# Six pairs of projection tiles in a hybrid decoder kernel: half-width block products in place of full tile products

## The chip, the cores and the metric

The kernel runs on one core of one Trainium2 chip. A core has TensorE (PE in the profile: matrix products from SBUF into the 8 banks of PSUM), VectorE (DVE), ScalarE (ACT), GpSimd (POOL) and SyncE (SP, which issues the weight transfers). Each engine works through its own instructions in order, and they meet through semaphores. The metric is the device time of one execution in microseconds (us), the median of several. Everything is float32.

## The reference, cut to what matters

Two decoder layers run over 256 prompt tokens and 32 sample tokens together, T = 288 columns. Each layer begins with one projection of the normalised input, `proj = h @ w_in`, with `h` of 288 x 1024 and `w_in` of 1024 columns in and some 9,000 out. Its columns are cut into the inputs of three token mixers:

```
hq, hf, hi, hg = jnp.split(proj[..., OFF_HG:OFF_SSM], 4, axis=-1)
fgate = lb + (1.0 - lb) * jax.nn.sigmoid(hf.astype(jnp.float32))
o_hg, s_hg = hgrn2_recurrence(heads(jax.nn.silu(hq)), heads(1.0 - fgate),
                              heads(jnp.log(fgate)), heads(hi), hg_s0)
y_hg = (rms_norm(o_hg, hg_norm) * jax.nn.silu(heads(hg).astype(jnp.float32)))
ssm = proj[..., OFF_SSM:OFF_ATT]
z = ssm[..., :SSM_WIDTH]
```

After the mixers come an output projection and a channel mixer: a dense one after layer 0, one of 8 experts after layer 1.

## The kernel before, in words

Features lie on the 128 partitions, tokens along the free axis. The input `hT` is 8 blocks of 128 features x 288 tokens. A projection tile `t` is 128 output features: 8 matmuls of 128x128 weights against 128x288 tokens, summed in one PSUM bank (`proj_tile`, L1078). Tiles 0 to 3 are hq, 4 to 7 hf, 8 to 11 hi, 12 to 15 hg, 16 to 19 z, 20 to 27 the convolved inputs, and so on up to tile 69. One weight slab of 1 MB holds two tiles; a ring of four slabs is refilled by SyncE when the second tile of a slab is done.

TensorE's order is written out: after the tile `t`, `small_products(L, t)` runs what belongs there. After tile 14 it turns hi into token rows (`value_rows`), after tile 15 it turns the convolution's state rows; after tiles 19, 21, 23, ... 33 come the products of the eight levels of the recurrence (`level`), and after tile 20 those of the level called "same".

ScalarE empties each bank in the order of the tiles (its `mixer`), and does the exponentials, logarithms and tanh in between. VectorE's order in this stretch is `hgrn_inputs` and then `hgrn_levels`. `hgrn_inputs` gates hq, adds 1 to exp(-hf) (`plus`, signal hg_plus), scales to the forget gate (four instructions), clamps it, waits for its logarithm, runs four cumulative sums, forms the first level's distances (`level_dist`), and gates hg. `hgrn_levels` is for each level `i`: two multiplications (signals lvl_q and lvl_k, for which TensorE's level `i` waits), the distances for level `i + 1`, from level 2 on a quarter of the convolution for one tile, and the masks that take the level's products out of PSUM. Level `i` begins when TensorE has done level `i - 1`. In layer 0, VectorE first builds masks and constants, before `hgrn_inputs`.

GpSimd does nothing between its setup and the end of the levels; then it forms the decayed keys (L943, L944), scales states (L951, L975) and weighs decays (L968).

The dense channel mixer of layer 0 already works in the way that the change brings to the projection: `fast_pair` (L1710) computes two tiles by seven products of half width, `put` being one matmul. There VectorE forms the sums of weight blocks.

Of the kernel before, what the change touches and what calls it, by code (L numbers as in the profile page):

```python
# [8 lines left out]
ALU = mybir.AluOpType  # L9
# [3 lines left out]
P = 128  # L13
# [54 lines left out]
GATE0 = 46  # L68
NKEY = 128 + 4 * 128 + 4 * 64 + AG * TS
# [24 lines left out]
def hybrid_decoder(nc, x_prompt, x_sample, state_hgrn, state_ssm, state_conv, cache_kv_w128, cache_kv_w512,  # L94
# [6 lines left out]
    with ctx:  # L101
# [35 lines left out]
        spread = view(over, 34 * T, 6, P)  # L137
# [191 lines left out]
        sums_done, tokens_ready, part_summed, part_kept = map(sem, ("sums_done", "tokens_ready", "part_summed", "part_kept"))  # L329
# [35 lines left out]
        def plan_mixer(L):  # L365
            job(("norm", L, 0), 0)
            for t in range(N_PROJ):
                acc_job(("proj", L, t))
# [160 lines left out]
        def sums_ready(i, k):  # L529
            return sums_done, 4 * min(i, N_PAIR) + 5 * max(i - N_PAIR, 0) + k  # L530
# [51 lines left out]
        def plan_slabs(L):  # L582
            for s in range(NS_HG + NS_SSM):
                add_slab(("proj", L, 2 * s + 1), (0, rows_of(w_in[L], 0, KT, 256 * s, 256)))
# [279 lines left out]
        def _(pool):  # L864
# [66 lines left out]
            for L in range(DEPTH):  # L931
# [8 lines left out]

                pool.wait_ge(*at("kd_decay", L))
                pool.wait_ge(*filled(("lvl", L, 7, 0)))
                step(gp.tensor_tensor(kt[:, :, 0:TP], hgp[:, 4:8, 0:TP], dist[:, :, 0:TP], ALU.mult))  # L943
                say(gp.tensor_tensor(fourfold(spread[:, 0:4, :]), tail_of(hgp[:, 4:8, :]), tail_of(dist), ALU.mult),  # L944
# [79 lines left out]
        def _(pe):  # L1024
# [61 lines left out]

            def proj_slab(L, keys, nk, src):
# [37 lines left out]
            def level(L, i):  # L1125
                if i == "same":
                    kk, qq = hgp[:, 4:8], hgp[:, 0:4]
                    pe.wait_ge(*at("hg_gated", L))
# [34 lines left out]
            def decayed_keys(L):  # L1163
                pe.wait_ge(*at("kd_ready", L))
                for b in range(3):
                    yield from token_rows(("kdtok", L, b), kt, b, range(HH), 0)
# [87 lines left out]
            def ssd_x_rows(L):  # L1254
                pe.wait_ge(*at("xs_ready", L))
                pe.wait_ge(*at("vexp_ready", L, 2))
                for b in range(3):
                    yield from token_rows(("xtok", L, b), xs, b, range(4), 0)

            def ssd_b_rows(L):  # L1260
# [11 lines left out]
                yield from token_rows(("btok", L, 2), xs, 2, (4, 5), 4)  # L1272
# [326 lines left out]
            def mixer(L):  # L1599
                for t in range(N_PROJ):  # L1600
                    run(proj_tile(L, t))
# [108 lines left out]
            def fast_pair(i, sums_of, b11, b21, b22):  # L1710
# [4 lines left out]
                h = KT // 2  # L1715

                def product(out, w, x, fresh):
                    for k in range(h):
                        ins = put(out, w[:, k, :], x[:, k, :], fresh and k == 0, k == h - 1)
                    return ins  # L1720
# [62 lines left out]
            def dense(L):  # L1783
# [16 lines left out]
                pe.wait_ge(tokens_ready, 1)  # L1800
# [4 lines left out]
                for q in range(KT // 2):  # L1805
                    for c, (k0, n) in enumerate(CHUNKS):
                        take_slab(4 * n, P)
                        if q == 0:
                            pe.wait_ge(tokens_ready, 2 + c)
# [161 lines left out]
        def _(act):  # L1971
# [218 lines left out]

            def mixer(L):
# [5 lines left out]
                for t in range(N_PROJ):  # L2197
# [13 lines left out]
                    elif t < 16:  # L2211
                        out = halve_out if t < 4 or t >= 12 else copy_out
                        if t == 11:
                            act.wait_ge(*filled(key))
                            step(fn(hgp[:, t, :], psum(key)[:, 0:T], ACT.Copy))
                            empty(fn(fourfold(spread[:, 0:4, :]), tail_of(hgp[:, 8:12, :]), ACT.Copy), key)
                        else:
                            out(hgp[:, t, :], key, psum(key)[:, 0:T])
                    elif t < 20:
                        halve_out(zT[:, t - 16, :], key, psum(key)[:, 0:T])  # L2220
# [20 lines left out]
                    if t == 15:  # L2241
                        say(fn(kt, hgp[:, 12:16, :], ACT.Tanh), "hg_exp", L, 3)
# [4 lines left out]
                    if t == 19:  # L2247
                        say(fn(zexp, zT, ACT.Tanh), "z_exp", L)
# [1121 lines left out]
```

## Time and profile before

| | |
|---|---|
| median of three runs | 2108.63 us (2107.93 to 2115.63) |
| the profiled execution | 2107.59 us, of which the span of the core is 2105.8 us |
| TensorE busy | 2071.3 us, 98% of the span |
| VectorE / ScalarE / GpSimd busy | 734.9 / 400.1 / 103.8 us |
| mixer of layer 0, tiles 2 to 35 | 29.7 to 178.9 us |
| the same of layer 1 | 734.0 to 881.3 us |
| dense channel mixer | about 500 to 729 us |
| experts | from about 1224 us |

The profile is one execution. Its parts are read like this: a row of the order of time has start, duration, engine, line and operation, what is written and what is read, the shapes, the count where equal instructions were merged, and in brackets the idle time in front and what ended it. PE MATMUL records come two to a matmul, since a float32 matmul is two instructions in the trace. Several instructions go through one line of a helper (L1042 for all matmuls, L2468 for all of VectorE's tensor_tensor, L1992 for ScalarE), so shapes tell them apart.

### The profile page before, as it was taken

The page shows a single profiled execution, that of the slowest core. Times are in us where ns is not written, and L with a number is a line of the kernel's source. Part 1 is how long each engine was busy: PE and PEld are TensorE (multiplying, and loading weights), DVE is VectorE, ACT ScalarE, POOL GpSimd, SP SyncE. Part 2 cuts the span into 40 slices and gives each one's busy share as a digit, 9 for nine tenths or more (in the row PEclk, how much of TensorE's full clock was granted, in tenths as well). Part 3 has the DMA queues.
Part 4 walks back from the last instruction along what each step waited for, and adds up shares of the span by engine and source line. Part 5 has one row for each costly group of instructions (what it writes and reads, how often), then busy time and mean ns, then how long its engine had stood idle before and what let it go on. Part 6 is the DMA issues. An engine that isn't in the chain of part 4 may idle for free.

```text
span 2105.8 us, 45046 instructions
## 1 busy us (share of the span) xinstructions
PE 2071.3 (98%) x19989; PEld 1326.1 (63%) x19989; DVE 734.9 (35%) x1437; ACT 400.1 (19%) x762; POOL 103.8 (5%) x160
## 2 busy tenths in 40 slices
PE   7999999999999999999999999999999999999998
PEld 5777777778999977777777734344443434343435
DVE  5386333545677627743254311010101010101013
ACT  3423424311220123334342120000000000000000
POOL 3001020000000000011200010000000000000001
PEclk9999999999999999999999999999999999999999
DMA  5434544785554443454466699999999999999996
GB/s 167 133 108 127 181 126 133 203 258 163 161 152 147 154 131 121 122 166 125 150 190 201 233 363 412 409 411 409 412 411 410 413 405 415 402 416 394 410 415 264
DMA packets 287990, 548.77 MB, mean 261 GB/s; under 512 B 12883, under 2 KB 218501, under 8 KB 271348
## 3 DMA queue, kind: packets, MB, share of 16 engines
q1 hardware_dynamic: 279808, 535.85, 70.5%
q10 hardware_dynamic: 6644, 5.58, 0.9%
q0 software_dynamic: 1344, 4.45, 0.5%
q8 instruction: 158, 2.59, 0.5%
q14 instruction: 36, 0.29, 0.0%
HBM read 527.15 MB, written 22.50 MB: 261 GB/s over the span
## 4 chain that ended last, share of the span: by engine, by line
PE 94%; DVE 2%; DMA 1%; issue 1%; POOL 1%; ACT 1%; POOLq 0%; DVEq 0%; ACTq 0%
PE bank L1042 91%; PE bank L1048 3%; DMA mem<-in_w_moe_down_dram 1%; ACT mem L1992 1%; DVE mem L2468 0%; DVE mem L2791 0%; DVE mem L2472 0%; DVE hflat L2501 0%; POOL quarterm L915 0%; DVE mem L2817 0%; POOL lmask L891 0%; POOL lmask L893 0%; DVE col L2824 0%; DVE hflat L2468 0%; DVE mem L2828 0%
## 5 line engine op out<-in xcount | busy, mean ns | idle before, releaser
L1042 PE MATMUL bank<-mem 128*32 128x256 f32 (+10 forms) x12904 | 1047.3, 390 | 13.0 <-issue 4.2
L1042 PEld LDWEIGHTS bank<-mem 128*32 128x32 f32 (+2 forms) x12904 | 636.1, 126 | 407.8 <-issue 234.5
L1042 PE MATMUL bank<-hflat,mem 128*128 128x288 f32 (+4 forms) x2784 | 629.0, 385 | 0.9 <-ACT hflat L1992 0.7
L1042 PEld LDWEIGHTS bank<-hflat,mem 128*128 128x128 f32 (+2 forms) x2784 | 479.4, 188 | 122.5 <-issue 12.2
L1992 ACT ACTIVATE mem<-bank 128x288 f32<-128x288 f32 (+5 forms) x411 | 174.0, 428 | 834.6 <-PE bank L1042 770.2
L1042 PE MATMUL bank<-mem,steps 128*32 128x384 f32 (+1 forms) x3072 | 289.8, 539 | 0.0
L1042 PEld LDWEIGHTS bank<-mem,steps 128*32 128x32 f32 x3072 | 94.8, 110 | 191.7 <-issue 190.9
L2468 DVE TENSOR_TENSOR mem<-mem 128x512 f32<-128x512 f32 (+10 forms) x280 | 191.8, 711 | 28.6 <-PE bank L1042 18.5
L2472 DVE SCALAR_TENSOR_TENSOR hflat<-hflat,bank 128x512 f32<-128x512 f32 x24 | 15.1, 683 | 410.5 <-ACT hflat L1992 410.5
L1992 ACT ACTIVATE hflat<-bank 128x512 f32<-128x512 f32 (+1 forms) x40 | 19.6, 553 | 562.9 <-PE bank L1042 562.9
L1992 ACT ACTIVATE mem<-mem 128x1152 f32<-128x1152 f32 (+7 forms) x127 | 93.4, 737 | 107.2 <-DVE mem L2546 71.6
L1048 PE MATMUL bank<-ident,mem 128*128 128x128 f32 (+3 forms) x503 | 70.9, 280 | 12.6 <-DMA mem<-in_x_sample_dram 7.4
L2472 DVE SCALAR_TENSOR_TENSOR mem<-mem,bank 128x288 f32<-128x288 f32 (+1 forms) x73 | 34.1, 486 | 138.1 <-ACT mem L1992 100.1
L1048 PEld LDWEIGHTS bank<-ident,mem 128*128 128x128 f32 (+3 forms) x503 | 58.1, 145 | 27.8 <-issue 11.9
L2475 DVE SCALAR_TENSOR_TENSOR mem<-mem,bank 128x384 f32<-128x384 f32 (+2 forms) x45 | 18.4, 438 | 107.6 <-PE bank L1042 106.9
L1992 ACT ACT_TABLE_LOAD x41 | 52.6, 1283 | 17.4 <-issue 11.1
L2468 DVE TENSOR_TENSOR mem<-mem,bank 128x256 f32<-128x256 f32 (+2 forms) x92 | 37.5, 407 | 34.7 <-PE bank L1042 32.3
L998 POOL DMA_INDIRECT mem<-yslots,mem x6 | 5.9, 978 | 836.7 <-PE bank L1042 835.2
L2475 DVE SCALAR_TENSOR_TENSOR hflat<-hflat,bank 128x512 f32<-128x512 f32 x24 | 15.1, 683 | 83.8 <-PE bank L1042 83.8
L2472 DVE SCALAR_TENSOR_TENSOR mem<-mem 128x288 f32<-128x288 f32 (+3 forms) x45 | 25.4, 565 | 27.7 <-ACT mem L1992 26.3
L2625 DVE SCALAR_TENSOR_TENSOR mem<-mem,vecs 128x312 f32<-128x312 f32 x48 | 26.1, 545 | 1.7
L2563 DVE COPY_PREDICATED mem<-lmask,bank 128x512 f32<-128x512 uint32 (+1 forms) x32 | 21.6, 675 | 11.7 <-PE bank L1042 10.7
(244 smaller groups left out, 676.7 us busy)
## 6 DMA issues: line engine op xcount, KB each, us to landing
mem<-in_w_moe_up_dram SPq DMA_DIRECT2D x64, 2048.0 KB, 20.9
mem<-in_w_moe_down_dram SPq DMA_DIRECT2D x56, 2048.0 KB, 21.9
mem<-in_w_moe_up_dram SPq DMA_DIRECT2D x32, 2304.0 KB, 22.8
mem<-in_w_in_dram SPq DMA_DIRECT2D x70, 1024.0 KB, 5.3
mem<-in_w_moe_up_dram SPq DMA_DIRECT2D x16, 1536.0 KB, 21.9
mem<-in_w_ffn_up_dram SPq DMA_DIRECT2D x44, 512.0 KB, 5.1
mem<-in_cache_kv_w_dram SPq DMA_DIRECT2D x26, 512.0 KB, 4.9
mem<-in_cache_kv_w_dram SPq DMA_DIRECT2D x74, 128.0 KB, 4.7
```

What stands on the lines that cost most here:

```text
L998: return gp.indirect_dma_start(dst, None, src, bass.IndirectOffsetOnAxis(ap=slots, axis=0), bounds_check=last_row, oob_is_err=False)
L1042: return mm(out, lhsT, rhs, start=start, stop=stop, skip_group_check=True)
L1048: return nc.tensor.transpose(out, in_, ident[0:k, 0:k])
L1992: return nc.scalar.activation(out, in_, f, **kw)
L2468: return ve.tensor_tensor(out, a, b, op)
L2472: return ve.scalar_tensor_tensor(out, tanh, 1.0, b, ALU.add, ALU.mult)
L2475: return ve.scalar_tensor_tensor(out, a, 0.5, b, ALU.mult, op)
L2563: empty(ve.copy_predicated(a[0:n], mk, src), key)
L2625: ins = ve.scalar_tensor_tensor(cv[:, m, 0:CW], xpad[:, m, j:j + CW], w[j], cv[:, m, 0:CW], ALU.mult, ALU.add)
```

## The change

For pairs 4 to 9 (tiles 8 to 19) the input features are cut into two halves of four blocks and the tokens into two halves of 144 (TH). A pair's weights are then a 2x2 array of blocks, w11, w12 (first feature half; first and second tile) and w21, w22, the inputs a 2x2 array too, and the 8 products of the plain way become 7:

```diff
+            def proj_pair(L, t):
+                p, h = t // 2, KT // 2
...
+                (a11, a12), (_, a22) = quarters(slab(n_slab[0], KT, 2 * P))
+                t1, t2, t3, t4 = (tok_m[:, j] for j in range(4))
+                s1, s2, s3, s4 = (msum[SEVEN.index(p) % 2][:, j] for j in range(4))
...
+                if t % 2 == 0:
+                    a = open_bank(("piece", L, p, 0))
+                    product(third(a, 0), a11, hT[:, 0:h, 0:TH], True)
+                    product(third(a, 1), a12, hT[:, h:KT, 0:TH], False)
+                    pe.wait_ge(*at("hg_plus", L, 1))
+                    close_bank(product(third(a, 2), a22, t4, False), ("piece", L, p, 0))
+                    pe.wait_ge(*mixer_sums(L, p, 1))
+                    product(third(open_bank(("piece", L, p, 1)), 0), s1, t1, True)
+                    return
+                b = psum(("piece", L, p, 1))
+                pe.wait_ge(*mixer_sums(L, p, 2))
+                product(third(b, 1), s2, t2, False)
+                pe.wait_ge(*mixer_sums(L, p, 3))
+                close_bank(product(third(b, 2), s3, t3, False), ("piece", L, p, 1))
+                c = open_bank(("piece", L, p, 2))
+                pe.wait_ge(*mixer_sums(L, p, 4))
+                close_bank(product(third(c, 0), s4, hT[:, h:KT, TH:T], True), ("piece", L, p, 2))
```

A `product` is four matmuls of 128x128 against 128x144. GpSimd forms the four sums of weight blocks of a pair, each 128x512, into one of two buffers. It starts on pair 4 when ScalarE has done the first tanh (hg_exp 1), and on pair p + 2 when TensorE has finished pair p:

```diff
+                for i, p in enumerate(SEVEN):
+                    n = first_slab[L] + p
+                    pool.wait_ge(slab_in[n % RING], 16 * slab_dmas[n])
+                    if i >= 2:
+                        pool.wait_ge(*filled(("piece", L, SEVEN[i - 2], 2)))
...
+                    if i == 0:
+                        pool.wait_ge(*at("hg_exp", L, 1))
+                    gp.tensor_tensor(s[0], w21, w22, ALU.add).then_inc(sums_done, 1)
+                    pool.wait_ge(*mixer_sums(L, p, 1))
+                    gp.tensor_tensor(s[1], s[0], w11, ALU.subtract).then_inc(sums_done, 1)
+                    gp.tensor_tensor(s[2], w11, w21, ALU.subtract).then_inc(sums_done, 1)
+                    pool.wait_ge(*mixer_sums(L, p, 2))
+                    gp.tensor_tensor(s[3], w12, s[1], ALU.subtract).then_inc(sums_done, 1)
+                    pool.wait_ge(*mixer_sums(L, p, 4))
```

ScalarE copies the seven pieces of a pair to SBUF, in three instructions (432, 432 and 144 columns) in place of two of 288. It may only write pair p + 2 when VectorE has joined pair p:

```diff
+            def keep_pieces(L, t):
...
+                if t % 2 == 0 and i >= 2:
+                    act.wait_ge(*pair_joined(L, SEVEN[i - 2]))
+                for piece in ((0,), (1, 2))[t % 2]:
+                    key, n = ("piece", L, p, piece), 1 if piece == 2 else 3
+                    out(parts[i % 2][:, 3 * piece:3 * piece + n, :].rearrange("p j t -> p (j t)"), key,
+                        psum(key)[:, 0:n * TH])
```

VectorE forms the four sums of input blocks (`pair_sums`, 128x576 each) after the first gating, and joins the pieces of each pair by five additions. Where the joins stand, and what else moves on VectorE:

```diff
+            def join_pair(L, p):
...
+                dve.wait_ge(*drained(("piece", L, p, 2)))
+                step(tt(s[:, 4], s[:, 4], s[:, 0], ALU.add))
+                step(tt(s[:, 5], s[:, 5], s[:, 4], ALU.add))
+                step(tt(dst[:, 1], s[:, 5:6].to_broadcast([P, 2, TH]), s[:, 2:4], ALU.add))
+                step(tt(s[:, 3], s[:, 3], s[:, 4], ALU.add))
+                ins = tt(dst[:, 0], s[:, 0:4:3], s[:, 1:7:5], ALU.add)
+                if p == 5:
+                    step(ins)
+                    ins = ve.tensor_copy(fourfold(spread_v), tail_of(hgp[:, 8:12, :]))
...
             def hgrn_inputs(L):
...
                 step(sigmoid_times(hgp[:, 0:4, :], qt, hgp[:, 0:4, :]))
+                h = KT // 2
+                pair_sums(tok_m, hT[:, 0:h, 0:TH], hT[:, 0:h, TH:T], hT[:, h:KT, 0:TH], hT[:, h:KT, TH:T])
...
+                join_pair(L, 4)
                 dve.wait_ge(*at("hg_log", L))
...
                 level_dist(L, 0)
-                dve.wait_ge(*at("hg_exp", L, 3))
-                say(sigmoid_times(hgp[:, 12:16, :], kt, hgp[:, 12:16, :]), "hg_gated", L)
-
+                join_pair(L, 5)
+                join_pair(L, 6)
...
+                join_pair(L, 7)
+                join_pair(L, 8)
...
                     if i == 0:
                         level_mask(L, "same")
-                    if i == 1:
+                        join_pair(L, 9)
+                        dve.wait_ge(*at("hg_exp", L, 3))
+                        say(sigmoid_times(hgp[:, 12:16, :], gate_temp, hgp[:, 12:16, :]), "hg_gated", L)
+                    if i == 3:
                         dve.wait_ge(*at("z_exp", L))
                         say(sigmoid_times(zT, zexp, zT), "z_gated", L)
```

TensorE's `value_rows` (after tile 14) waits for the join of pair 5 instead of ScalarE's copies; its level "same" waits for lvl_k 1 instead of the gating of hg; ScalarE's tanh of hg moves from tile 15 to tile 17, that of z from 19 to 22. Buffers are moved to make room, and in the dense part one semaphore is replaced by others that say the same.

On GpSimd, between the setting to zero of three arrays and the decayed keys of layer 0, before:

```order
L937 MEMSET mem 128x512
L938 MEMSET mem 128x512
L939 MEMSET mem 32x128
L943 TENSOR_TENSOR mem<-mem 128x4x256
L944 TENSOR_TENSOR mem<-mem 128x512
```

and after the change:

```order
L959 MEMSET mem 128x512
L960 MEMSET mem 128x512
L961 MEMSET mem 32x128
L972 TENSOR_TENSOR mem<-mem 128x512
L974 TENSOR_TENSOR mem<-mem 128x512
L975 TENSOR_TENSOR mem<-mem 128x512
L977 TENSOR_TENSOR mem<-mem 128x512
L972 TENSOR_TENSOR mem<-mem 128x512
```

Twenty-four sums (the last four lines stand six times) now lie in a stretch in which GpSimd had none.

On VectorE, from the gating of hq in layer 0 (the first row) to the first level's distances, before:

```order
L2472 SCALAR_TENSOR_TENSOR mem<-mem 128x1152
L2479 TENSOR_SCALAR mem<-mem 128x1152
L2513 TENSOR_SCALAR mem<-mem,lb 128x288 x4
L2515 TENSOR_SCALAR mem<-mem 128x1152
L2516 TENSOR_SCALAR mem<-mem 128x1152
L2519 SCALAR_TENSOR_TENSOR mem<-reset,mem 128x288 x4
L2468 TENSOR_TENSOR mem<-mem 128x1152
L2546 SCALAR_TENSOR_TENSOR mem<-mem 128x1152
```

and after the change:

```order
L2549 SCALAR_TENSOR_TENSOR mem<-mem 128x1152
L2545 TENSOR_TENSOR mem<-hflat 128x576 x2
L2545 TENSOR_TENSOR mem<-hflat,mem 128x576 x2
L2556 TENSOR_SCALAR mem<-mem 128x1152
L2609 TENSOR_SCALAR mem<-mem,lb 128x288 x4
L2611 TENSOR_SCALAR mem<-mem 128x1152
L2612 TENSOR_SCALAR mem<-mem 128x1152
L2545 TENSOR_TENSOR mem<-mem 128x144 x2
L2545 TENSOR_TENSOR mem<-mem 128x288
L2545 TENSOR_TENSOR mem<-mem 128x144
L2545 TENSOR_TENSOR mem<-mem 128x288
L2616 SCALAR_TENSOR_TENSOR mem<-reset,mem 128x288 x4
```

The four sums of inputs come in front of hg_plus (now L2556), and a join in front of the cumulative sums (now L2616); the join of pair 5 follows the first level's distances.

On VectorE, from the masks of "same" to the multiplications of level 1, before:

```order
L2563 COPY_PREDICATED mem<-ident,bank 128x512 x2
L2563 COPY_PREDICATED mem<-ident,bank 32x128
L2468 TENSOR_TENSOR mem<-mem 128x1152 x3
L2546 SCALAR_TENSOR_TENSOR mem<-mem 128x1152
```

and after the change:

```order
L2661 COPY_PREDICATED mem<-ident,bank 128x512 x2
L2661 COPY_PREDICATED mem<-ident,bank 32x128
L2545 TENSOR_TENSOR mem<-mem 128x144 x2
L2545 TENSOR_TENSOR mem<-mem 128x288
L2545 TENSOR_TENSOR mem<-mem 128x144
L2545 TENSOR_TENSOR mem<-mem 128x288
L2549 SCALAR_TENSOR_TENSOR mem<-mem 128x1152
L2545 TENSOR_TENSOR mem<-mem 128x1152 x3
```

The join of pair 9 and the gating of hg now stand between the masks and the two multiplications for which TensorE's level 1 waits.

## Rows read from the trace of the kernel before

**Rows 1.** The page: busy digits of 40 slices, TensorE and VectorE.
```profile
PE   7999999999999999999999999999999999999998
DVE  5386333545677627743254311010101010101013
```
**Rows 2.** Order of time, layer 0: copies of tiles 12 and 13; dense mixer: one product.
```profile
72.75 0.41 ACT L1992 ACTIVATE mem<-bank 128x288 f32<-128x288 f32 x1 [0.33 <-PE bank L1042]
76.63 0.41 ACT L1992 ACTIVATE mem<-bank 128x288 f32<-128x288 f32 x1 [3.47 <-PE bank L1042]
...
518.67 1.14 PE L1042 MATMUL bank<-hflat,mem 128*128 128x144 f32 x8
...
525.53 1.14 PE L1042 MATMUL bank<-hflat,mem 128*128 128x144 f32 x8
```
**Rows 3.** Order of time, layer 1, from tile 7's copy to the cumulative sums.
```profile
757.58 0.41 ACT L1992 ACTIVATE mem<-bank 128x288 f32<-128x288 f32 x1 [3.47 <-PE bank L1042]
...
759.29 0.76 DVE L2479 TENSOR_SCALAR mem<-mem 128x1152 f32<-128x1152 f32 x1 [14.16 <-ACT mem L1992]
...
766.93 1.83 DVE L2513 TENSOR_SCALAR mem<-mem,lb 128x288 f32<-128x288 f32 x4 [6.88 <-ACT mem L1992]
...
776.75 3.13 DVE L2519 TENSOR_TENSOR_SCAN mem<-reset,mem 128x288 f32<-128x288 f32 x4 [6.41 <-ACT mem L1992]
```
**Rows 4.** Order of time, layer 0: first tanh, and VectorE's constants up to the gating.
```profile
38.28 1.16 ACT L1992 ACTIVATE mem<-mem 128x1152 f32<-128x1152 f32 x1
...
39.68 0.29 DVE L3125 TENSOR_SCALAR amask<-amask 128x256 f32<-128x256 f32 x1
...
49.01 1.36 DVE L2472 SCALAR_TENSOR_TENSOR mem<-mem 128x1152 f32<-128x1152 f32 x1
```
**Rows 5.** Groups by line and shape: count, then busy us and mean ns.
```profile
L944 POOL TENSOR_TENSOR mem<-mem 128x512 f32<-128x512 f32 x2 | 2.5, 1260 | 0.2
L2468 DVE TENSOR_TENSOR mem<-mem 128x144 f32<-128x144 f32 x20 | 6.1, 307 | 0.7
L2468 DVE TENSOR_TENSOR mem<-mem 128x288 f32<-128x288 f32 x28 | 12.8, 458 | 1.0
L2468 DVE TENSOR_TENSOR mem<-mem 128x576 f32<-128x576 f32 x10 | 7.6, 758 | 0.3
```
**Rows 6.** Order of time, where GpSimd and VectorE meet, layer 0.
```profile
172.76 2.36 POOL L943 TENSOR_TENSOR mem<-mem 128x1024 f32<-128x1024 f32 x1 [147.88 <-ACT mem L1992]
...
173.40 1.86 DVE L2468 TENSOR_TENSOR mem<-mem 128x128 f32<-128x128 f32 x1
...
175.19 1.26 POOL L944 TENSOR_TENSOR mem<-mem 128x512 f32<-128x512 f32 x1
...
175.30 1.33 DVE L2622 TENSOR_SCALAR mem<-mem,vecs 128x312 f32<-128x312 f32 x1
...
179.28 0.44 DVE L2622 TENSOR_SCALAR mem<-mem,vecs 128x312 f32<-128x312 f32 x1
...
196.24 0.42 DVE L2595 COPY mem<-bank 128x256 f32<-128x256 f32 x1 [1.63 <-PE bank L1042]
196.37 1.91 POOL L951 TENSOR_TENSOR mem<-mem 128x1024 f32<-128x1024 f32 x1 [19.92 <-PE bank L1042]
```
**Rows 7.** Order of time, layer 0: after "same", level 1, and level 4.
```profile
110.24 4.15 PE L1042 MATMUL bank<-hflat,mem 128*128 128x288 f32 x16
...
111.14 4.21 DVE L2468 TENSOR_TENSOR mem<-mem 128x1152 f32<-128x1152 f32 x3
...
114.32 0.99 PE L1042 MATMUL bank<-mem 128*32 128x32 f32 x72
...
141.65 0.75 PE L1042 MATMUL bank<-mem 128*32 128x32 f32 x64 [0.67 <-issue]
```
**Rows 8.** Stretches: PE, PEld, DVE, ACT, POOL busy, granted clock, DMA share, GB/s.
```profile
1220.00:1223.00 3.00, 2.52 (x55) 1.46 (x59) 0.08 (x1) 0.00 (x0) 0.00 (x0) 0.73 1.02 423
1223.00:1226.00 3.00, 2.14 (x19) 0.49 (x22) 0.00 (x0) 2.51 (x4) 0.00 (x0) 0.50 0.79 322
```

More of the change, by code:

```diff
@@ L136, in hybrid_decoder @@
         hgp = view(over, 18 * T, 16, T)
-        spread = view(over, 34 * T, 6, P)
+        spread_v = view(arena, 13784, 4, P)
+        spread_x = view(arena, 17280, 6, P)
+        tok_m = view(over, 34 * T, 4, KT // 2, TH)
+        msum = [view(over, 2048 * i, 4, KT // 2, P) for i in range(2)]
+        parts = [view(over, 42 * T + 7 * TH * i, 7, TH) for i in range(2)]
+        gate_temp = view(arena, 14720, 4, T)
         yall = view(over, 42 * T, 10, T)
@@ L367, in plan_mixer @@
             for t in range(N_PROJ):
-                acc_job(("proj", L, t))
+                if t // 2 not in SEVEN:
+                    acc_job(("proj", L, t))
+                elif t % 2 == 0:
+                    for i in range(3):
+                        acc_job(("piece", L, t // 2, i))
                 if t == AT_VTOK:
@@ L1085, in proj_tile, with product @@
                     yield
+            def product(out, w, x, fresh):
+                for k in range(KT // 2):
+                    ins = put(out, w[:, k, :], x[:, k, :], fresh and k == 0, k == KT // 2 - 1)
+                return ins
+            def proj_pair(L, t):
+                p, h = t // 2, KT // 2
+                if t % 2 == 0:
+                    take_slab(KT, 2 * P)
+                (a11, a12), (_, a22) = quarters(slab(n_slab[0], KT, 2 * P))
+                t1, t2, t3, t4 = (tok_m[:, j] for j in range(4))
+                s1, s2, s3, s4 = (msum[SEVEN.index(p) % 2][:, j] for j in range(4))
+                third = lambda acc, i: acc[:, TH * i:TH * i + TH]
+                if t % 2 == 0:
+                    a = open_bank(("piece", L, p, 0))
[14 more added lines that the diff above has]
+                close_bank(product(third(c, 0), s4, hT[:, h:KT, TH:T], True), ("piece", L, p, 2))
+                n_slab[0] += 1
             def proj_slab(L, keys, nk, src):
@@ L1271, in ssd_b_rows @@
                     yield
[L1272 removed]
+                yield from token_rows(("btok", L, 2), xs, 2, (4, 5), spread_x[:, 4:6])
             def row_to(n, width):
@@ L1600, in mixer @@
                 for t in range(N_PROJ):
-                    run(proj_tile(L, t))
+                    if t // 2 in SEVEN:
+                        proj_pair(L, t)
+                    else:
+                        run(proj_tile(L, t))
                     if t == 0:
@@ L2210, in mixer @@
                         act.wait_ge(*drained(key))
[L2211 to L2220, printed above, removed]
+                    elif t // 2 in SEVEN:
+                        keep_pieces(L, t)
+                    elif t < 8:
+                        out = halve_out if t < 4 else copy_out
+                        out(hgp[:, t, :], key, psum(key)[:, 0:T])
                     elif t < 28:
```

80 lines of the change are left out of this document (47 added, 33 removed).

## The prediction, written before the changed kernel ran

> **What bounds the kernel now.** I read the page first: TensorE is busy in nine tenths and more of every slice but the first and the last [rows 1], so time that TensorE is spared, or made to wait, is time of the kernel. VectorE is far from full over the span, but not in the slices of the two mixers [rows 1]. Then I read the order of time in the mixers, since the shares are means. Up to tile 19 VectorE waits for ScalarE more than it works: in layer 1 it idles 14.2, 6.9 and 6.4 us ahead of hg_plus, the scaling and the cumulative sums [rows 3]. From level 1 on it does not idle at all and TensorE is at its heels: the two multiplications of level 1 begin at 111.14, and TensorE, which needs them, comes at 114.1 and starts at 114.32; at level 4 it waits 0.67 [rows 7]. So a saving in tiles 8 to 19 reaches the end only if VectorE keeps up until level 1. GpSimd has nothing to do there before.
>
> **TensorE's work.** A tile takes 76.63 - 72.75 = 3.88 us [rows 2], a pair 7.76. The dense mixer runs the same seven products: the same product returns after 525.53 - 518.67 = 6.86 us [rows 2], 0.98 a product. The pair gets 0.90 shorter, six pairs 5.4 us, two layers 10.8 us. That is the most the change can bring, if no wait comes in its place.
>
> **What one sum on GpSimd costs VectorE.** A sum reads two SBUF operands of 128x512; the row of that shape says 1.26 us [rows 5], four to a pair 5.3 us with gaps, less than the 6.9 us of a pair; and GpSimd is two pairs ahead, so TensorE does not wait for the sums themselves. But the trace shows what such an instruction does to VectorE [rows 6]. A subtraction of 128 columns took 1.86 us, until 0.14 after the end of GpSimd's L943; a 128x312 tensor_scalar that otherwise takes 0.44 took 1.33 beside GpSimd's L944. A copy from PSUM at 196.24 went through GpSimd's L951 at its usual 0.42. So VectorE instructions on SBUF stand still until GpSimd's current one ends. When both have work they alternate: each sum holds VectorE about 1.26 - 0.19 - 0.08 = 1.0 us (the held subtraction ended 0.14 us after GpSimd did, and a free one of that size takes more: it gets in about 0.19 before the end; 0.08 is my estimate for the time in which GpSimd is between two sums). Bounds for this price: 0 (all hidden), and 1.26. I take 1.0, the row of the same shape.
>
> The Trainium skill has this as a rule ("SBUF — State Buffer", Who interferes with whom): GpSimd shares a port pair with VectorE, and a VectorE instruction with two SBUF inputs, or in a two-port mode, and a GpSimd one that reads SBUF exclude each other for a whole instruction. It exempts VectorE instructions with one SBUF input outside those modes. The row at 175.30 is one tensor and scalars, at 0.44 us for 312 columns no fast mode, and was held: there the row goes further than the rule. By the rule, the four scalings (L2513) would run free, and the total below would be about 3 us less.
>
> **Term 1, TensorE waits for hg_plus.** The third product of pair 4 now waits for it, since the input sums are made in front of it. Layer 1: tile 7's copy begins at 757.58, so tile 8 at 757.2 and the third product at 759.2; hg_plus ends at 760.05 [rows 3]. The four input sums (4 x 0.79 with gaps [rows 5]) are covered by the 14.2 us in which VectorE idles in front of it, even if each is held. Wait 0.9. Layer 0: the tanh ends at 39.44, GpSimd starts its first eight sums (pairs 4 and 5, whose slabs replace those of tiles 0 to 3, done by 37.6) and VectorE is in its constants from 39.68 to 49.0, 37 short instructions back to back [rows 4]. Eight holds of 1.0 move the gating from 49.0 to 57.0; it takes 1.4, the input sums 3.15, hg_plus 0.8: 62.3. TensorE is there at 72.75 - 5 x 3.88 - 0.4 + 1.96 = 54.9. Wait 7.4. If the constants aren't held it is 0.9 (constants end at 49.0, gating and input sums at 53.5, before ScalarE's exponential is there).
>
> **Term 2, TensorE waits after tile 14 for the join of pair 5.** Count from hg_plus, X. TensorE: five products of pair 4 (4.9), pairs 5 and 6 (13.7), four products of pair 7 (3.9): X + 22.5. ScalarE's sigmoid is ready at X + 6.9 (760.05 to 766.9 [rows 3]). The cumulative sums need the logarithm, and that needs ScalarE to be done with pair 5. Before, they began at 776.75, 4.0 after TensorE ended tile 11 (757.2 + 4 x 3.88); ScalarE's copy of the sample columns falls away from these, about 0.7 with the rest, so 3.3 after pair 5 (X + 11.8): X + 15.1. Without holds VectorE has joined pair 4 by then (a join is 3 x 0.307 + 2 x 0.458 and gaps, 2.0 [rows 5]), then cumulative sums 3.1 [rows 3], distances 2.75 (two instructions of the kind of which three take 4.21 [rows 7]), join 2.0 and a copy of 512 columns, 0.6 by estimate from the 0.76 for 576 [rows 5]: X + 23.5, wait 1.0. With holds: GpSimd's sums of pairs 6, 7 and 8 start as TensorE ends pairs 4, 5 and 6 (X + 5.3, 12.2, 19.1), twelve of them. Three fall on the scalings, one on the second clamp, three on the join of pair 4, which ends at X + 19.1, and four on the cumulative sums, which end at X + 26.2. Distances to X + 29.0, join and copy to X + 31.6. TensorE is there at X + 23.6, since ScalarE may not empty pair 6's first bank before pair 4 is joined: emptied at 19.1 + 0.6, wanted at 18.6. Together 9.1 us in each layer; without holds 1.0.
>
> **Term 3, level 1.** TensorE ends "same" at 110.24 and VectorE began its multiplications 0.90 later [rows 7]. Now the join of pair 9 (2.0) and the gating (1.4) stand between: 0.9 + 3.4 + 2.75 = 7.05 after "same", and TensorE's tile 21 takes 3.88. Wait 3.2 against 0.2: 3.0 more in each layer. This needs no holds, GpSimd being done. Behind it the gating of z moves two levels down, so levels 2 and 3 wait less and level 4 0.2 more than its 0.67; by then both chains are where level 1 put them, 0.2 more.
>
> ScalarE's third copy and GpSimd's delay of nothing else cost nothing: ScalarE has idle time ahead of each copy (3.47 us [rows 2]), and the joins of pairs 6 to 8 are done while TensorE makes pairs 7 to 9. Should that cover fail, level 0 waits too, up to 2 us in a layer; that is in the range. The weight ring is freed a little earlier or later with TensorE, at one 1 MB slab in 6.9 us, with no wait on slabs in these stretches.
>
> **Sum.** Layer 0: -5.4 + 7.4 + 9.1 + 3.0 + 0.2 = +14.3. Layer 1: -5.4 + 0.9 + 9.1 + 3.0 + 0.2 = +7.8. Together +22.1 us on the profiled execution's 2107.59: 2129.7. That execution is 1.0 below the median of the runs, so 2130.7, in round numbers 2131.
>
> **Rivals.**
> First, the two engines don't hold each other up as in [rows 6], or only now and then. Then layer 0 is -5.4 + 0.9 + 1.0 + 3.0 + 0.2 = -0.3, layer 1 the same: 2108. For it: only a handful of instructions meet in the whole trace. Against it: each SBUF one that did was held.
>
> Second, the stalls make TensorE's clock fall. Where TensorE had 0.99 and 0.86 us gaps amid small products, three us were granted 0.73 and three 0.50 [rows 8]. My stalls are 7 to 8 us, three of them; 0.27 x 3 + 0.50 x 3 is 2.3 us of lost work, I say 3 with the way back, 10 in all: 2141. Against it: the waits of the mixers in this trace pass at full clock, but none is longer than 2 us. The Trainium skill says the same way ("TensorE: Matmul & The Clock Gate", Part 1): idle falls to 1.2 GHz, and full rate comes back only after a while of work.
>
> Third, faster: every wait is covered and the 10.8 us stay, 2098. The place is the join of pair 5 and level 1: it needs the join by X + 22.5, which with no holds is missed by 1.0, and VectorE's 7.05 us after "same" to be under 3.88. Only a much quicker VectorE would do it; its rows say otherwise.
>
> **Chances and range.** As computed, 0.62 (its own range 2119 to 2141: low end with constants and scalings not held and shorter holds, high end with holds of 1.26 us); clock falling too, 0.15; no holds, 0.19; faster 0.04. The range from 2107 to 2144 takes in the first three. What can be told from no change is about 0.5%, 10.5 us. Slower by more: 0.62 + 0.15, 0.77; within: 0.19; faster: 0.04.
>
> **What would show it.** Right: VectorE's instructions beside L972 to L977 of the new kernel last a microsecond longer than their shapes do; hg_plus near 62 in layer 0; TensorE waits of about 7, 8 and 3 us at pair 4 of layer 0, after tile 14, and at level 1, and pairs otherwise at 6.86. Wrong: VectorE's durations there as ever (then 2108), or GpSimd's sums taking over 1.8 us, so that TensorE waits for them (then over 2144).

## The result, and the profile after

The changed kernel takes 2132.89 us (median of 6, 2131.54 to 2136.76) against 2110.42 (6 runs, 2107.93 to 2115.63): ratio 1.011, 95% interval 1.0099 to 1.012. Forecast were 2131 and a range of 2107 to 2144. The profiled execution took 2131.73 us, 24.1 more than the one of before. The lines below are from this execution.

The page's busy digits have a 7 for TensorE in slices 2 and 16 of 40, in the two mixers, where 9 stood before [rows 1]:

```profile
PE   7799999999999997999999999999999999999998
DVE  5787342544677557943244321010101010101013
```

TensorE's waits (line waited for: us in total, times, longest). L2596 is the copy behind the join of pair 5, issue mostly level 1, L2556 hg_plus:

```profile
PE bank L1087 <- DVE mem L2596: 14.2, 2, 7.2
PE bank L1081 <- issue: 7.5, 4, 3.6
...
PE bank L1081 <- DVE mem L2556: 6.5, 2, 5.9
```

TensorE in order of time, layer 0 (the third product of pair 4, the turning of tiles 8 to 11, level 0, level 1 and the tiles behind it, level 7):

```profile
60.83 6.91 PE L1081 MATMUL bank<-mem 128*128 128x144 f32 x32 [5.87 <-DVE mem L2556]
...
93.83 2.82 PE L1087 MATMUL bank<-ident,mem 128*128 128x128 f32 x12 [7.15 <-DVE mem L2596]
...
114.25 2.32 PE L1081 MATMUL bank<-mem 128*128 128x128 f32 x24
...
129.88 0.99 PE L1081 MATMUL bank<-mem 128*32 128x32 f32 x72 [3.00 <-issue]
130.79 9.72 PE L1081 MATMUL bank<-hflat,mem 128*128 128x288 f32 x32
...
186.35 1.13 PE L1081 MATMUL bank<-mem 128*128 128x128 f32 x8
```

Level 1 stood at 114.32 before [rows 7], so the layer is 15.6 late there; at level 7 it is 16.2 late (170.13 before). Layer 1 adds 8.7 (level 7 from 872.53 to 897.48), with the same two waits; what follows is 0.8 shorter than before:

```profile
807.06 2.82 PE L1087 MATMUL bank<-ident,mem 128*128 128x128 f32 x12 [7.10 <-DVE mem L2596]
...
841.36 1.46 PE L1081 MATMUL bank<-mem 128*32 128x32 f32 x72 [3.63 <-issue]
```

What holds VectorE. GpSimd and VectorE in layer 0's constants (before, the cast took 0.29 and the gating began at 49.01 [rows 4]):

```profile
39.36 1.33 POOL L972 TENSOR_TENSOR mem<-mem 128x512 f32<-128x512 f32 x1 [14.88 <-ACT mem L2059]
39.60 1.24 DVE L3218 TENSOR_SCALAR mem<-mem 128x256 int32<-128x256 int32 x1
40.77 1.27 POOL L974 TENSOR_TENSOR mem<-mem 128x512 f32<-128x512 f32 x1
40.87 1.31 DVE L3219 CAST mem<-mem 128x256 f32<-128x256 int32 x1
...
48.65 1.32 POOL L977 TENSOR_TENSOR mem<-mem 128x512 f32<-128x512 f32 x1
48.87 0.15 DVE L3237 TENSOR_SCALAR mem<-mem 128x1 int32<-128x1 int32 x1
...
55.45 1.36 DVE L2549 SCALAR_TENSOR_TENSOR mem<-mem 128x1152 f32<-128x1152 f32 x1
```

Each VectorE instruction ends just after GpSimd's current one. Then the chain from hg_plus to the join of pair 5 (scalings, join 4, cumulative sums, the two distances, join 5, copy), and last the join of pair 7, beside the sums of pair 9:

```profile
60.01 0.76 DVE L2556 TENSOR_SCALAR mem<-mem 128x1152 f32<-128x1152 f32 x1
68.80 5.47 DVE L2609 TENSOR_SCALAR mem<-mem,lb 128x288 f32<-128x288 f32 x4 [8.03 <-ACT mem L2059]
...
75.89 5.87 DVE L2545 TENSOR_TENSOR mem<-mem 128x144 f32<-128x144 f32 x5
81.79 4.91 DVE L2616 TENSOR_TENSOR_SCAN mem<-reset,mem 128x288 f32<-128x288 f32 x4
86.73 2.24 DVE L2545 TENSOR_TENSOR mem<-mem 128x1152 f32<-128x1152 f32 x1
89.00 2.30 DVE L2644 SCALAR_TENSOR_TENSOR mem<-mem 128x1152 f32<-128x1152 f32 x1
91.34 1.97 DVE L2545 TENSOR_TENSOR mem<-mem 128x144 f32<-128x144 f32 x5
93.35 0.43 DVE L2596 COPY mem<-mem 128x512 f32<-128x512 f32 x1
...
101.00 5.08 DVE L2545 TENSOR_TENSOR mem<-mem 128x144 f32<-128x144 f32 x5
```

Free times are 1.83 for the scalings and 3.13 for the cumulative sums [rows 3], 1.98 for a join and 1.36 for each distance (trace of e1_memset): 3.6 + 3.9 + 1.8 + 0.9 + 0.9 = 11.1 us of standing still. In layer 1 the same rows give 2.4 + 3.9 + 2.7 + 0.9 + 0 = 9.8. The join of pair 5 falls into a time in which GpSimd is idle, and is free.

### The profile page after: what moved, and what is told of

The parts are those of the page before. It is cut to its first block, busy times and chain, and to the rows that moved or that the text cites. A ratio compares the mean times of both kernels' runs of the same rounds, so it can differ in the third digit from the quotient of the medians.

```text
span 2130.0 us, 45811 instructions
## 1 busy us (share of the span) xinstructions
PE 2069.5 (97%) x20277; PEld 1378.3 (65%) x20277; DVE 801.4 (38%) x1507; ACT 404.9 (19%) x772; POOL 172.1 (8%) x208
## 4 chain that ended last, share of the span: by engine, by line
PE 89%; DVE 6%; DMA 1%; ACT 1%; issue 1%; POOL 1%; POOLq 0%; DVEq 0%; ACTq 0%
PE bank L1081 86%; PE bank L1087 3%; DVE mem L2545 2%; DMA mem<-in_w_moe_down_dram 1%; ACT mem L2059 1%; DVE mem L2616 0%; DVE mem L2609 0%; DVE mem L2549 0%; DVE hflat L2578 0%; ACT L2059 0%; DVE mem L2892 0%; POOL quarterm L937 0%; DVE mem L2644 0%; DVE mem L2918 0%; DVE mem L2661 0%
## 5 line engine op out<-in xcount | busy, mean ns | idle before, releaser
L1081 PE MATMUL bank<-mem 128*32 128x256 f32 (+9 forms) x13288 | 1099.8, 387 | 25.7 <-issue 7.5
L1081 PEld LDWEIGHTS bank<-mem 128*32 128x32 f32 (+3 forms) x13288 | 714.1, 128 | 393.5 <-issue 221.9
L1081 PE MATMUL bank<-hflat,mem 128*128 128x288 f32 (+3 forms) x2688 | 575.9, 373 | 1.5 <-ACT hflat L2059 0.7
L1081 PEld LDWEIGHTS bank<-hflat,mem 128*128 128x128 f32 (+2 forms) x2688 | 445.0, 189 | 104.9 <-issue 13.1
L2059 ACT ACTIVATE mem<-bank 128x288 f32<-128x288 f32 (+10 forms) x423 | 180.1, 430 | 841.6 <-PE bank L1081 748.4
L2545 DVE TENSOR_TENSOR mem<-mem 128x512 f32<-128x512 f32 (+10 forms) x340 | 229.5, 696 | 32.7 <-PE bank L1081 18.9
L1081 PEld LDWEIGHTS bank<-mem,steps 128*32 128x32 f32 x3072 | 102.8, 110 | 183.6 <-issue 181.3
L2059 ACT ACTIVATE mem<-mem 128x1152 f32<-128x1152 f32 (+9 forms) x125 | 92.1, 738 | 111.7 <-DVE mem L2644 76.4
L1029 POOL TENSOR_TENSOR mem<-mem 128x288 f32<-128x288 f32 x16 | 12.7, 793 | 207.8 <-DVE mem L2549 207.5
```

Of the source, the lines that this page charges most:

```text
L1029: say(gp.tensor_tensor(gates[:, m, :], gates[:, m, :], gates[:, 8 + m, :], ALU.add), "two_summed", L, m + 1)
L1081: return mm(out, lhsT, rhs, start=start, stop=stop, skip_group_check=True)
L2059: return nc.scalar.activation(out, in_, f, **kw)
L2545: return ve.tensor_tensor(out, a, b, op)
```

## The experiments

Times are medians, the ratio is to the kernel before, timed beside it, with its 95% interval. The part of an execution behind level 7 of layer 1, which no edit touches, takes between 1232.5 and 1237.2 us in the traces of this case, so differences of medians of a few us are checked against the trace below. All runs at a glance:

| kernel | us | ratio |
|---|---|---|
| changed kernel | 2132.9 | 1.011 (1.0099 to 1.012) |
| e1_memset | 2107.8 | 0.9986 (0.9977 to 0.9996) |
| e8_copy | 2111.5 | 0.9995 (0.9985 to 1.0004) |
| e2_join5 | 2119.5 | 1.0038 (1.0024 to 1.0052) |
| e3_join9 | 2136.0 | 1.0118 (1.0101 to 1.0135) |
| e4_tok | 2131.5 | 1.0093 (1.0076 to 1.011) |
| e7_fill | 2132.4 | 1.0092 (1.0074 to 1.011) |
| e5_joins | 2116.6 | 1.0023 (1.0011 to 1.0034) |
| e10_gpsimd_again | 2110.6 | 0.9999 (0.999 to 1.0009) |
| e6_vector_sums | 2100.0 | 0.9944 (0.9926 to 0.9962) |
| e9_z5 | 2097.4 | 0.9937 (0.9919 to 0.9955) |
| e11_vector_sums, e12_z5 (both again) | 2099.0, 2100.5 | 0.9947 (0.9933 to 0.9961), 0.9951 (0.9937 to 0.9964) |

### e1_memset: GpSimd without the reading

```diff
-                    gp.tensor_tensor(s[0], w21, w22, ALU.add).then_inc(sums_done, 1)
+                    gp.memset(s[0], 0.0).then_inc(sums_done, 1)
```

and so for the other three.

> GpSimd writes zeros over its 48 buffers of 128x512 in place of forming the sums of weight blocks (the projection's six pairs are then not the reference's); every wait and signal stays. My theory: it is GpSimd's reading that holds VectorE. The setting to zero of this size takes 0.52 us and reads nothing, so the constants of layer 0, scalings, join 4, cumulative sums and distances take their free times (scalings 1.83, join 2.0, cumulative sums 3.13, distances 1.36 each), TensorE's waits at pair 4 and after tile 14 fall to about 1, and only level 1's of 3 us with the clock behind it stays: about 2111. Rival, the time comes from VectorE's added work and its order: 2133 as after the change. Rival, GpSimd's writing holds VectorE as well, 0.5 us each: about 2120.

2107.75: 25 us gone, 3 more than I said. Order of time, layer 0: TensorE at pair 4, VectorE's scalings and join 4, TensorE after tile 14, the join of pair 7 beside the memsets of pair 9, and TensorE at level 1:

```profile
55.63 4.19 PE L1081 MATMUL bank<-mem 128*128 128x144 f32 x32 [0.67 <-DVE mem L2556]
...
62.56 1.98 DVE L2609 TENSOR_SCALAR mem<-mem,lb 128x288 f32<-128x288 f32 x4 [6.99 <-ACT mem L2059]
...
66.17 1.98 DVE L2545 TENSOR_TENSOR mem<-mem 128x144 f32<-128x144 f32 x5
...
79.07 1.53 PE L1087 MATMUL bank<-ident,mem 128*128 128x128 f32 x12 [0.63 <-DVE mem L2596]
...
84.64 1.97 DVE L2545 TENSOR_TENSOR mem<-mem 128x144 f32<-128x144 f32 x5
84.73 0.53 POOL L975 MEMSET mem<- 128x512 f32 x1
...
113.52 1.46 PE L1081 MATMUL bank<-mem 128*32 128x32 f32 x72 [3.00 <-issue]
```

The rival of added work and order falls: both are still there, and the two waits are not. They are 0.67 and 0.63, where the prediction's case without holds had 0.9 and 1.0. Level 1's 3.0 us is untouched, so it is a cost of its own. A shorter instruction of GpSimd would explain a part of this too, and for the constants it does: those beside a memset (0.52) still take 0.57 in place of 0.29, and the gating begins at 49.95. But the join of pair 7, which stood still beside sums (5.08), goes at its free 1.97 beside memsets: for these additions it is the reading.

### e8_copy: one operand read in place of two

```diff
-                    gp.tensor_tensor(s[0], w21, w22, ALU.add).then_inc(sums_done, 1)
+                    gp.tensor_copy(s[0], w21).then_inc(sums_done, 1)
```

> GpSimd copies one block of 128x512 in place of each sum (the projection's six pairs are then not the reference's): one operand read in place of two. My theory: what holds VectorE is GpSimd's reading SBUF, one operand or two, until its instruction ends. If a copy lasts about 0.9 us, VectorE's instructions beside it last some 0.65 longer: about 2120. Rival, one-operand instructions of GpSimd go beside VectorE: no row held, 2108 as with the setting to zero.

2111.54. The copies take 0.61, less than I had supposed, and hold VectorE as long as they last:

```profile
39.51 0.61 POOL L972 COPY mem<-mem 128x512 f32<-128x512 f32 x1 [14.74 <-ACT mem L2059]
...
39.56 0.70 DVE L3228 TENSOR_SCALAR amask<-amask 128x256 f32<-128x256 f32 x1
...
86.46 2.76 DVE L2545 TENSOR_TENSOR mem<-mem 128x144 f32<-128x144 f32 x5
```

The last row is the join of pair 7 again: 1.97 beside memsets, 2.76 beside copies of nearly the same length, 5.08 beside sums. So one operand read is enough, and between a copy and a sum the price goes by the duration of GpSimd's instruction. The gating begins at 50.91: later than 49.95, much sooner than 55.45.

### e2_join5: the join of pair 5 ahead of the logarithm

```diff
                 join_pair(L, 4)
+                join_pair(L, 5)
                 dve.wait_ge(*at("hg_log", L))
...
                 level_dist(L, 0)
-                join_pair(L, 5)
                 join_pair(L, 6)
```

> Only the join of pair 5 (with its copy) moves, from behind the first level's distances to directly behind the join of pair 4, ahead of the wait for the logarithm. The holds stay. My theory: the wait after tile 14 is the cumulative sums and distances standing in front of this join. In layer 1 the join of pair 4 ends 18.7 us after hg_plus, a held join of 5.0 and the copy follow: 24.2, and TensorE is there at 23.6. The waits of 7.15 and 7.10 fall under 1.5, and the clock stays up there, some 2 us more in each layer: 2133 - 17 = 2116. The waits at pair 4 (5.9) and level 1 (3.0 and 3.6) stay. Rival, VectorE is simply full: the later cumulative sums make level 0 or the masks late and TensorE waits there instead: 2128 or more.

2119.46, 13.4 gained of the 17 expected, with no instruction taken away; by the trace 6.1 in layer 0 and 6.0 in layer 1. The wait after tile 14 is 0.52 and 1.41, and level 0 doesn't wait. What is missing: in layer 0 hg_plus ended at 62.3 and not 60.8 in this execution (eight constants were held, not seven), a wait of 7.08; TensorE waits 1.29 and 0.41 at pair 9, for copies that ScalarE may make only after the join of pair 6, now held (4.83 in layer 0); and in layer 1 the way from level 1 to level 4 is 0.95 longer.

### e3_join9: work moved out of level 0, into levels 1 and 2

```diff
-                        join_pair(L, 9)
-                        dve.wait_ge(*at("hg_exp", L, 3))
-                        say(sigmoid_times(hgp[:, 12:16, :], gate_temp, hgp[:, 12:16, :]), "hg_gated", L)
+                    if i == 2:
+                        dve.wait_ge(*at("hg_exp", L, 3))
+                        say(sigmoid_times(hgp[:, 12:16, :], gate_temp, hgp[:, 12:16, :]), "hg_gated", L)
...
+                    if i == 1:
+                        join_pair(L, 9)
```

with the tanh of z at tile 24. By then the convolution has overwritten the tanh of hg, so that hg is not gated as in the reference.

> Only the work between the masks of level 0 and the multiplications of level 1 moves: the join of pair 9 stands behind the distances made in level 1, the gating of hg in level 2, the tanh of z at tile 24. My theory: the waits at level 1 (3.0 and 3.6 us) go to 0.2, with them the clock's fall there (the tiles behind take 9.72 and 8.95 where 8.03 is usual, the level's products 0.99 and 1.46), and the waits of 0.67 at later levels come back: 2133 - 9 = 2124. Rival, VectorE is behind by then as a whole and the moved instructions only make levels 2 and 3 wait: 2130 to 2133.

2136.03. I was wrong and the rival right. TensorE at levels 1, 3 and 4:

```profile
127.73 1.00 PE L1081 MATMUL bank<-mem 128*32 128x32 f32 x72
...
147.69 0.75 PE L1081 MATMUL bank<-mem 128*32 128x32 f32 x64 [2.06 <-issue]
...
158.47 0.75 PE L1081 MATMUL bank<-mem 128*32 128x32 f32 x64 [2.07 <-issue]
```

Level 1 starts without a wait, and level 4, at 158.47, later than the 157.90 of the changed kernel. From level 1 to 4 VectorE has no idle time at all: what is put there is paid there.

### e4_tok: the wait at pair 4 taken away alone

```diff
-                pair_sums(tok_m, hT[:, 0:h, 0:TH], ...)
...
                 if L == 0:
                     lower_bounds()
...
-                    pe.wait_ge(*at("hg_plus", L, 1))
+                    pe.wait_ge(*at("tok_ready", L))
```

with the input sums directly behind tiles 0 and 1, and ScalarE waiting for hg_plus ahead of pair 4's first copy.

> VectorE forms the sums of the inputs before the constants and the gating, with a signal of their own, for which TensorE waits at pair 4 in place of hg_plus. My theory: the 5.9 us wait at pair 4 in layer 0 goes, and nothing is won: hg_plus itself is as late as before (60.8), the join of pair 5 follows it by 32.6 us, so that TensorE begins the turning of tile 8 to 11 at 93.8 as before, after a longer wait (16 us, part of it on banks): 2133, within 2. Rival, the waits add up and each one removed is won: 2133 - 8.7 (5.9 and 2.8 of slow clock) = 2124.

2131.48. A wait of 5.9 us is gone and 1.4 gained, the time that I expected. TensorE now waits one pair later for ScalarE, and still after tile 14 for the join of pair 5:

```profile
63.89 4.18 PE L1081 MATMUL bank<-hflat,mem 128*128 128x144 f32 x16 [3.79 <-ACT mem L2059]
...
90.93 2.82 PE L1087 MATMUL bank<-ident,mem 128*128 128x128 f32 x12 [6.22 <-DVE mem L2598]
```

But the rows don't stand where I put them. hg_plus ended at 63.1, not 60.8, and the join of pair 5 with its copy 27.8 behind it, not 32.6: TensorE had finished pair 4 early, so that GpSimd's sums of pair 6 no longer met the scalings. The turning begins 2.9 earlier. At level 7 of layer 1 this execution is 3.6 ahead (893.86 against 897.48), and its rest is 4.7 longer, so that the median hides a gain. It is still less than the 8.7 of the rival.

### e7_fill: TensorE kept busy through its waits

```diff
+                keep_busy(("vtok", L, 0), 18 if L == 0 else 14)
                 pe.wait_ge(*pair_joined(L, 5))
```

and so at pair 4 of layer 0 and level 1.

> The changed kernel, in which TensorE passes its waits with products of 128x288 whose result is overwritten: 12 ahead of the wait for hg_plus in layer 0, 18 and 14 ahead of the wait for the join of pair 5, 6 ahead of level 1 in each layer. They take 0.485 us each, so they end just before the waits do. My theory: TensorE's clock falls because it stands still, and the falls cost what the slow rows show only where TensorE bounds afterwards: 1.6 us after tile 14 (20.4 us from the turning to level 0, where e1_memset takes 18.8) and 0.7 behind level 1 in each layer; behind hg_plus nothing, since the wait after tile 14 takes it back. 2133 - 4.6 = 2128.3, with the clock at 1.00 in all of the mixer. Rival, all slow rows count (2.8 behind hg_plus as well, 1.9 and 1.6 behind level 1): 2123.5. Rival, the fall has another cause than idleness: clock and time as after the change, 2133.

The clock in windows of the changed kernel's layer 0 (PE, PEld, DVE, ACT, POOL busy, granted clock, DMA share, GB/s):

```profile
59.00:62.00 3.00, 1.17 (x5) 1.17 (x6) 1.70 (x3) 0.00 (x0) 0.00 (x0) 0.60 0.00 0
62.00:65.00 3.00, 3.00 (x14) 3.00 (x14) 0.00 (x0) 1.77 (x2) 0.00 (x0) 0.50 0.02 5
65.00:68.00 3.00, 3.00 (x21) 3.00 (x20) 0.00 (x0) 2.96 (x4) 0.00 (x0) 0.76 0.00 0
```

and the same view of e7_fill:

```profile
62.00:65.00 3.00, 2.55 (x20) 2.55 (x21) 0.40 (x1) 1.18 (x2) 0.00 (x0) 1.00 0.00 0
```

The fall to 0.50, the lower of the two levels (1.2 GHz), comes of standing still, and is gone. But 2132.43 and not 2128.3. TensorE's way from the turning to level 0 takes 18.8 and 18.9 in place of 20.4 and 20.6, as expected. Behind level 1 nothing is won: level 4 waits 1.75 for VectorE. And in layer 0 the products that fill the wait ran on after it was over:

```profile
92.85 0.43 DVE L2608 COPY mem<-mem 128x512 f32<-128x512 f32 x1
...
94.73 1.47 PE L1094 MATMUL bank<-ident,mem 128*128 128x128 f32 x12
```

The copy behind the join was done at 93.28, the turning began 1.4 later, and layer 0 keeps only 0.7 (level 7 at 185.62 against 186.35). In layer 1, where the products ended in time, the way from hg_plus to level 7 takes 119.5 in place of 121.1. So the falls cost 1.6 us a layer behind tile 14, by the trace; the median moved by 0.5, too little to show it.

### e5_joins: the join of pair 9 and the gating into VectorE's gap

As e2_join5, and:

```diff
                     if i == 0:
-                        level_mask(L, "same")
                         join_pair(L, 9)
                         dve.wait_ge(*at("hg_exp", L, 3))
                         say(sigmoid_times(hgp[:, 12:16, :], gate_temp, hgp[:, 12:16, :]), "hg_gated", L)
+                        level_mask(L, "same")
```

> GpSimd still forms the sums. The join of pair 5 stands ahead of the logarithm as in e2_join5, and the join of pair 9 with the gating of hg stands between the masks of level 0 and those of the level called same, where VectorE idled 4.1 us waiting for TensorE (e3_join9 and e1_memset show that gap) and has 3.4 us to do. My theory, corrected by e3_join9: from level 1 on VectorE is full and work moved further down is paid there, but work moved into this gap is free. Level 1's waits of 3.0 and 3.6 go to 0.2 and the clock stays up: 2119.5 - 8 = 2111.5. Rival, VectorE's load is what counts wherever it stands: 2119.

2116.61, 2.9 gained of 8. In layer 0 level 1's wait is 0.23 (3.01 in e2_join5), but level 4 waits 1.79 where it waited 0.29; in layer 1 level 1 still waits 2.70. The gap of 4.1 us is one of layer 0: in layer 1 level 0 and "same" take TensorE 1.00 us each in place of 2.32. VectorE bounds here too.

### e6_vector_sums and e10_gpsimd_again: who forms the sums

```diff
+                pair_weights(L, 4)
                 step(sigmoid_times(hgp[:, 0:4, :], qt, hgp[:, 0:4, :]))
                 dve.wait_ge(*at("hg_exp", L, 2))
                 plus(dist, "hg_plus", L, 1)
+                pair_weights(L, 5)
+                pair_weights(L, 6)
...
                 join_pair(L, 4)
+                pair_weights(L, 7)
                 join_pair(L, 5)
```

`pair_weights` is `four_sums`, the dense mixer's helper, on the pair's slab; those of pairs 8 and 9 stand behind joins 6 and 7. GpSimd's loop is gone. Joins as in e5_joins, input sums as in e4_tok.

> As e5_joins, but VectorE forms the sums of weight blocks itself (24 of 128x512 in a layer, some 0.67 us each by the 0.76 of 128x576) and GpSimd none; the sums of the inputs stand ahead of the constants and have a signal of their own. My theory: a sum on GpSimd costs VectorE 1.0 us of standing still, more than the 0.67 that it would cost there, and only when both have work; on VectorE it can be put into idle time. No instruction of VectorE is held any more, X is near 57.5, the waits at pair 4, after tile 14 and at level 1 stay under 1: 2107.75 (e1_memset) less 7 for level 1 = 2101, faster than before the change. Rival: 16 us more work in a layer makes VectorE late for join 5 or level 0 by 3 us and more: 2107 or above.

2099.98, as forecast, and 0.56% below the kernel before. VectorE's four sums of a pair, then TensorE at tile 14, level 1 and level 4:

```profile
52.12 2.62 DVE L2530 TENSOR_TENSOR mem<-mem 128x512 f32<-128x512 f32 x4
...
77.98 1.47 PE L1070 MATMUL bank<-ident,mem 128*128 128x128 f32 x12
...
109.30 0.99 PE L1064 MATMUL bank<-mem 128*32 128x32 f32 x72
...
136.63 0.75 PE L1064 MATMUL bank<-mem 128*32 128x32 f32 x64 [1.08 <-issue]
```

In layer 1 level 1 still waits 1.60 and level 4 1.43. A sum takes VectorE 0.66 with its gap, and its busy time over the span is 794.7 us, less than the 801.4 of the changed kernel although it does 48 instructions more: held time counts as busy.

> As e6_vector_sums (joins of pairs 5 and 9 moved, sums of the inputs ahead of the constants with a signal of their own), but GpSimd forms the sums of weight blocks again. It tells the placement of VectorE's work from the engine that sums. My theory: the holds make the difference. Constants with eight holds and the input sums in front end hg_plus near 63, the two joins end 25 after it, level 1 follows without a wait: as e5_joins or half a us above, 2117. Rival, the placement is what won and the engine matters little: 2105 or less.

2110.63: with VectorE's other work in the same places, the engine that sums is worth 10.6 us of the 32.9 between the changed kernel and e6_vector_sums. But my 2117 was 6 too high. In e4_tok taking the wait at pair 4 away won 1.4 (3.6 at level 7 of layer 1); here, with join 5 moved, it wins 6.0 over e5_joins (5.05 by the traces at the same place). TensorE gets to the end of pair 4 while the gating is still to come, so GpSimd's sums of pair 6 begin at 60.28. The first runs beside the gating and hg_plus, the others in VectorE's idle time, and the scalings are free:

```profile
60.28 2.24 POOL L972 TENSOR_TENSOR mem<-mem 128x512 f32<-128x512 f32 x1 [10.21 <-PE bank L1081]
...
68.80 1.83 DVE L2609 TENSOR_SCALAR mem<-mem,lb 128x288 f32<-128x288 f32 x4 [5.67 <-ACT mem L2059]
...
84.17 1.47 PE L1087 MATMUL bank<-ident,mem 128*128 128x128 f32 x12
```

### e9_z5, e11_vector_sums and e12_z5: the gating of z two levels further down

```diff
-                    if i == 3:
+                    if i == 5:
                         dve.wait_ge(*at("z_exp", L))
```

> As e6_vector_sums, with the gating of z (1.36 us with its gap 1.39) two levels further down, in level 5 in place of level 3. My theory: from level 1 to level 4 VectorE bounds (TensorE waits 1.08 and 1.43 at level 4), and from level 5 on TensorE does, so VectorE has time for it there: each layer gains its wait at level 4, 2100 - 2.5 = 2097.5. Rival, the wait comes back at level 6 or 7, or the median can't tell: 2100.

2097.44 (2096.55 to 2100.73), the time that I expected, but not for my reason. Level 4 waits in neither layer; at level 7 the wait is back in both:

```profile
165.15 1.13 PE L1064 MATMUL bank<-mem 128*128 128x128 f32 x8 [1.14 <-issue]
...
864.06 1.13 PE L1064 MATMUL bank<-mem 128*128 128x128 f32 x8 [1.48 <-issue]
```

e6_vector_sums is there at 165.09 and 864.06. So both kernels ran once more, on one chip.

> The kernel of e6_vector_sums, side by side with that of e9_z5 on one chip. In the traces both reach level 7 of layer 0 at 165.1 and of layer 1 at 864.06, so e9_z5 wins nothing by its own account, yet its median was 2.5 lower. My theory: that is the spread between chips or calls; side by side the medians agree within 1 us, both 0.55 to 0.6% below the kernel before.

> The kernel of e9_z5, side by side with that of e6_vector_sums. Rival to the theory of e11_vector_sums: the gating of z in level 5 wins 2.5 us somewhere behind the levels, then this one is 2 to 3 us below e11_vector_sums again.

2099.02 and 2100.45: the 2.5 us are gone, and the place of z's gating makes no difference that can be told. Both stay 0.5% below the kernel before, with intervals that leave no change out. VectorE bounds up to level 7.

## Why the prediction was right

- **TensorE's work.** Pairs run at 6.86 us where nothing is waited for. In e6_vector_sums, with 0.19 us of waits up to level 1, layer 0 is 5.0 ahead there (109.30 against 114.32); the steps have 5.4.
- **The price of a hold.** 1.0 us: a constant 0.29 to 1.24, join 4 3.9 longer by four. That it is GpSimd's reading is shown for the additions of a join (5.08 beside sums, 2.76 beside copies, 1.97 beside memsets); the constants were held by a memset too, as long as it lasted.
- **Term 1.** 5.9 and 0.66 against 7.4 and 0.9. Of eight sums only seven met a constant of size; the eighth ran beside instructions of 128x1, which took their usual 0.15. In e2_join5 all eight met one, and the wait is 7.1.
- **Term 2.** 7.15 and 7.10 against 9.1, which counted two waits, 8.0 here and 1.1 at pair 7 for ScalarE; that one was 0.5 in layer 1, and about 0.3 in layer 0 (three products in 3.42 in place of 3.10). The join of pair 5 and its copy end 33.0 after hg_plus in layer 0, 30.7 in layer 1, against 31.6; with hg_plus 1.5 earlier the turning begins at 93.83 where the steps give 93.9. There two errors cancel, which is luck. Eleven holds were forecast, 11.1 us measured in layer 0 and 9.8 in layer 1, though not spread as I said: in layer 0 the scalings lost 3.6 in place of 3, join 4 3.9 in place of 3, the cumulative sums 1.8 in place of 4, the distances 1.8 in place of nothing, the clamp nothing in place of 1.
- **Term 3.** 3.00 and 3.63 against 3.2; e1_memset shows that it needs no holds. Its cause was only half seen: VectorE is full through levels 1 to 4, so that level 1's wait can't be cured by moving work down (e3_join9). Level 4's term came out as 0.7 in layer 0 (28.0 from level 1 to level 4, 27.3 before) and 0 in layer 1, against 0.2.
- **What the sum lacked.** The clock's fall, set at nothing: 2.8 us behind pair 4 of layer 0, swallowed by the next wait; 1.6 behind tile 14 in each layer, paid (e7_fill); behind level 1 nothing, VectorE being later. The steps' +14.3 and +7.8 came out as +16.2 and +8.7. Of the 2.8 between, 3.2 are this; 0.5 (level 4, layer 0) and 0.4 (level 1, layer 1) more, and less 0.9 (join 5, layer 1) and twice 0.2 (level 1, layer 0, and level 4, layer 1), make up the rest. The rival of the clock was right about the fall and put its price at 10, where by the trace VectorE's chain leaves 3.
- **The Trainium skill's exemption** of VectorE instructions with one SBUF input and no fast mode ("SBUF — State Buffer", Who interferes with whom) would have let the scalings run free. They took 5.47 and 4.24 for 1.83, so the row of before was the better guide, and the 3 us less by the rule would have been wrong.

## What to carry to other kernels

An idle GpSimd is not free help for VectorE: while it read SBUF here, VectorE stood still for most of that time wherever it had work of size, and a sum that costs VectorE 0.66 us on its own queue cost it 1.0 on GpSimd's, at moments that nobody chose. Price such a helper by the rows in which both engines meet, and place VectorE's own work into its idle gaps instead. A wait of TensorE is worth only what the next one behind it leaves: find the chain that ends last, here join 5, and move that one first.

## What was not expected of the hardware

- The exclusion works both ways. GpSimd's sums take 1.26 alone, up to 2.41 (layer 1, at 760.41) when a long VectorE instruction is under way (the gating of 128x1152, 1.36, from 760.35).
- A GpSimd instruction that only writes (memset, 0.52) still doubled VectorE's 0.29 constants to 0.57, but left the additions of a join at their 1.97.
- Instructions of 128x1 (0.15) ran beside a sum without any delay.
